# The end of a two-layer block: who finishes the last eight tiles of the feed-forward, and how the last store is issued

## The chip, the cores and the metric

One NeuronCore of a Trainium2 chip runs the whole program. The metric is the device time of one execution in microseconds (us), as the median of several executions. The engines are TensorE (PE in the rows, its weight loads PEld), VectorE (DVE), ScalarE (ACT), GpSimd (POOL) and SyncE (SP, which here only issues DMAs). Each engine takes its instructions strictly in the order in which they are written.

## The reference, cut to what matters

Two transformer-like layers on 1024 tokens of width 1024, all in float32. The change touches only the very end of the second layer, the feed-forward and its norm:

```python
h = rmsnorm(x, pre_ffn_norm[l])
f = (silu(h @ ffn_w_gate[l]) * (h @ ffn_w_up[l])) @ ffn_w_down[l]
x = x + rmsnorm(f, post_ffn_norm[l])      # f * 1/sqrt(mean(f*f) + eps) * weight
```

## The kernel before

The tokens lie in eight tiles of 128. `layer2_ffn` computes the down product as seven block products of a Strassen-like scheme, each with 11 steps, so 77 steps in all (`STEPS_B`, numbered 0 to 76). A step loads two blocks of 128x512; ScalarE rounds both to the short format (`split_step`, lines 3699 and 3700, which raise `r_hi`), VectorE makes the two remainders (`low_step`, line 3982 and the one after it, shown in the profile as line 3742, which raise `r_lo`), and TensorE runs three groups of four matmuls. A group needs both high parts, the second group the first remainder, the third group the second remainder (lines 4163 to 4168). For steps 0 to 73 the order is step by step. The last three steps (74, 75, 76) are run tile by tile: nine matmuls for tile 0, then nine for tile 1, and so on (lines 4170 to 4178, semaphore `tile_done`). Tile 0 thus needs the splits and remainders of all three last steps.

Tiles 4 to 7 of the output (`OUT_ORDER` puts them first) get their last sums from product 5, on VectorE during steps 69 to 72. Tiles 0 to 3 get theirs from the last product, when `tile_done` says so. For each tile the work of the norm is then:

- the last sum, out of PSUM, on VectorE (line 4054, in the profile 3742, written to `features_T`, which the code calls `f`);
- the square and its sum along the row on ScalarE (`square`, line 3704), and the mean on VectorE (`mean`, line 4011);
- the multiplication by the norm weights on VectorE in halves of 512 columns (`weighted`, and line 4057 for the last half; out and in are `features_T`, the other input is `ff_gain`);
- the square root on ScalarE (`root`, line 3723), the reciprocal on VectorE (`inverse`, line 4016);
- the finish: scaling by the reciprocal and adding the residual, one instruction on VectorE over 1024 columns (`finish`, line 4024, x = f * r + x);
- the store of 512 KB by SyncE (line 3590), in the order `STORE_ORDER`.

ScalarE's order at the end is: both splits of a step, then a square or a root where one is due, then the splits of the next step. VectorE's is: the remainders of a step, then a sum, a mean, a weighting. `finish(0)` stands between the remainders of step 72 and those of step 73. All other finishes come after the remainders of step 76. GpSimd has done nothing since the middle of the feed-forward's start (line 4083).

Of the kernel before, what the change touches and what calls it, by code (L numbers as in the profile page):

```python
# [22 lines left out]
D = 1024  # L23
# [3369 lines left out]
def layer2_ffn(nc, block, mixed, W, B, G, U0, hT_hi, hT_lo, feat, st, x_in, g_post, out, a_dram, w_dram):  # L3393
# [4 lines left out]
    with ExitStack() as ctx:  # L3398
# [50 lines left out]
        def ring_raw(n):  # L3449
# [10 lines left out]
        r_here = [sem(f"r_here{s}") for s in range(R)]  # L3460
        r_hi, r_lo, step_done, tile_done = (sem(n) for n in ("r_hi", "r_lo", "step_done", "tile_done"))
        p1_b, evac_b = sem("p1_b"), sem("evac_b")
        x_here, sq_a, sq_b, ms, rt, scaled, x_new = (
            sem(n) for n in ("x_here", "sq_a", "sq_b", "ms", "rt", "scaled", "x_new"))
        x_t = x_in.rearrange("(t p) d -> t p d", p=P)
        out_t = out.rearrange("(t p) d -> t p d", p=P)

# [19 lines left out]
        FRESH = (True, True, False, True, True, False, False)  # L3487
        TILE_STEPS = 3
        OUT_ORDER = [4, 5, 6, 7, 0, 1, 2, 3]
        STORE_ORDER = [4, 5, 0, 6, 1, 7, 2, 3]  # L3490
        SCALED = [8, 10, 13, 16, 12, 15, 18, 20]

        def in_order(eng, start, pair, end):
            start()
# [8 lines left out]
        def _(sp):  # L3503
# [73 lines left out]
            def end():  # L3577
                for n in range(STEPS_B):
                    load_step(n)
                    if n == 7:  # L3580
                        spill(LAST, 0)
                    if n == 12:
                        sp.wait_ge(prod, 7 * H0 + 14 * LAST)
                        sp.dma_start(gain[:], g_post.to_broadcast([P, D])).then_inc(x_here, 16)
                    if n >= 13 and n % 2 and n < 13 + 2 * NT:
                        t = (n - 13) // 2
                        sp.dma_start(x[:, t, :], x_t[t]).then_inc(x_here, 16)
                for n, t in enumerate(STORE_ORDER):
                    sp.wait_ge(x_new, n + 1)
                    sp.dma_start(out_t[t], x[:, t, :]).then_inc(stored, 16)  # L3590
                sp.wait_ge(stored, 32 * PAIRS + 16 * NT)

            in_order(sp, start, pair, end)

# [1 line left out]
        def _(act):  # L3596
# [123 lines left out]
            def root(n):  # L3720
                t = OUT_ORDER[n]
                act.wait_ge(ms, n + 2)
                act.activation(st[:, t, 4:5], st[:, t, 3:4], ACT.Sqrt).then_inc(rt, 1)

            def end():
                for n in range(STEPS_B):
                    split_step(n)
                    p, t = divmod(n - PAIRS - 3, PAIRS)
                    if p >= 0 and t < 4:
                        piece(p, t)  # L3730
                    if p == 5 and 2 <= t < 6:
                        root(t - 2)
                for t in range(4):
                    act.wait_ge(evac_b, B_C12 + t + 1)
                    square(f[:, t, HALF:], t, 2, sq_b)
                    root(4 + t)

            in_order(act, start, pair, end)

        @block.vector  # L3740
        def _(dve):
# [271 lines left out]
            def inverse(n):  # L4013
                t = OUT_ORDER[n]
                dve.wait_ge(rt, n + 1)
                dve.reciprocal(st[:, t, 5:6], st[:, t, 4:5]).then_inc(scaled, 1)

            def weighted(t, at):
                TT(f[:, t, at:at + HALF], f[:, t, at:at + HALF], gain[:, at:at + HALF], ALU.mult).then_inc(scaled, 1)

            def finish(n):
                t = OUT_ORDER[n]
                dve.wait_ge(scaled, SCALED[n])
                dve.scalar_tensor_tensor(x[:, t, :], f[:, t, :], st[:, t, 5:6], x[:, t, :], ALU.mult, ALU.add).then_inc(x_new, 1)  # L4024

            def end():
                c12(1, LAST, 0)
                for k in (3, 1, 2, 4):
                    own_sum(k, LAST, 0)
                for n in range(R, STEPS_B):  # L4030
                    low_step(n)
                    p, t = divmod(n - PAIRS - 3, PAIRS)
                    if p >= 0 and t < 4:
                        piece(p, t)
                    if p == 4 and 4 <= t < 8:
                        dve.wait_ge(sq_a, t + 1)
                        weighted(t, HALF)
                    if p == 4 and t == 8:
                        dve.wait_ge(sq_a, NT)
                        dve.tensor_scalar(st[:, :, 1:2], st[:, :, 0:1], 1.0 / D, EPS, ALU.mult, ALU.add).then_inc(ms, 1)  # L4040
                        dve.wait_ge(ms, 1)
                    if p == 5 and 1 <= t < 5:
                        mean(t - 1)
                        weighted(3 + t, 0)
                    if p == 5 and t == 3:
                        inverse(0)
                        finish(0)
                for t in range(5):
                    if 1 <= t < 4:
                        inverse(t)  # L4050
                        finish(t)
                    if t < 4:
                        dve.wait_ge(tile_done, t + 1)
                        TT(f[:, t, HALF:], banks[0][t], u2_b[:, t, :], ALU.add).then_inc(evac_b, 1)
                    if t:
                        mean(3 + t)
                        TT(f[:, t - 1, HALF:], f[:, t - 1, HALF:], gain[:, HALF:], ALU.mult).then_inc(scaled, 1)
                        inverse(3 + t)
                        finish(3 + t)

            in_order(dve, start, pair, end)

# [1 line left out]
        def _(pool):  # L4064
# [16 lines left out]
            TT(own[0], own_block(0, 1), own_block(0, 0), ALU.subtract).then_inc(own_done, 1)  # L4081
            pool.wait_ge(own_done, 3)
            TT(own[2], own_block(1, 0), own[0], ALU.subtract).then_inc(own_done, 1)

        @block.tensor
        def _(pe):
# [249 lines left out]
```

## Time and profile before

| what | value |
|---|---|
| time, median of 3 runs | 2253.35 us (2251.65 to 2255.38) |
| span of the profiled execution (first to last instruction) | 2258.5 us |
| TensorE busy | 2216.4 us, 98% of the span |
| VectorE busy | 1581.9 us, 70% |
| ScalarE busy | 914.2 us, 40% |
| GpSimd busy | 263.5 us, 12% |
| mean granted TensorE clock | 0.990 |

The busy shares are means over the whole program. The profile gives the span of the profiled execution and no other time for it; that span is 5.15 us longer than the median of the runs. The times in the rows below count from the start of the span.

### The profile page before, as it was taken

Reading aid. Unit: us, or ns where it says so; the run is one execution under the profiler, and the core shown is the slowest. Engines: PE = TensorE matmul, PEld = TensorE weight load, DVE = VectorE, ACT = ScalarE, POOL = GpSimd, SP = SyncE. Lnnn points to the kernel's source line nnn. Section 1 sums busy time; section 2 is a strip of 40 time slices with the busy share of each in tenths; the row PEclk is TensorE's granted clock in tenths of the full one; section 3 lists DMA queues with packets and bytes.
Section 4 is the critical chain, followed back from the end, with each engine's and each line's share of the span. In section 5 each row is a group of like instructions: output and inputs, shape, how many; then the busy total and the mean of one; then the engine's idle time right before and its main releaser. Section 6 shows DMA issues by size and latency. Waiting matters only on the chain. (4 is left out here: it accounts for less than half of the span.)

```text
span 2258.5 us, 34288 instructions
## 1 busy us (share of the span) xinstructions
PE 2216.4 (98%) x13052; PEld 1823.0 (81%) x13052; DVE 1581.9 (70%) x2212; ACT 914.2 (40%) x1672; POOL 263.5 (12%) x266
## 2 busy tenths in 40 slices
PE   8999999999999999999999989999999999999997
PEld 7888888888888887887877777887888888888886
DVE  5657678876665545657687788887798777765557
ACT  5443544343343321243344445555533333324444
POOL 0222232100000000001232222322020000000000
PEclk9999999999999999999999989999999999999999
DMA  4111111144333264433233442323235444448655
GB/s 152 47 38 58 37 56 38 66 147 157 116 114 111 86 261 175 150 111 122 85 112 112 150 141 72 107 93 112 96 131 191 163 158 163 158 156 299 214 181 184
DMA packets 106952, 289.06 MB, mean 128 GB/s; under 512 B 9692, under 2 KB 35388, under 8 KB 102332
## 3 DMA queue, kind: packets, MB, share of 16 engines
q1 hardware_dynamic: 106812, 287.14, 36.2%
q8 instruction: 94, 1.54, 0.3%
q14 instruction: 46, 0.38, 0.1%
HBM read 205.01 MB, written 82.10 MB: 127 GB/s over the span
## 5 line engine op out<-in xcount | busy, mean ns | idle before, releaser
L124 PE MATMUL psG<-h_hi,w_hi 128*128 128x512 f32 (+1 forms) x624 | 164.4, 395 | 2.1 <-DVE features_T L1875 1.6
L124 PE MATMUL psG<-h_hi,w_lo 128*128 128x512 f32 (+1 forms) x624 | 161.6, 391 | 0.0
L124 PE MATMUL psG<-h_lo,w_hi 128*128 128x512 f32 (+1 forms) x624 | 161.4, 392 | 0.0
L455 POOL TENSOR_TENSOR sb_w<-sb_left 128x128 f32<-128x128 f32 (+3 forms) x96 | 96.9, 1014 | 320.3 <-DVE sb_left L582 320.3
L124 PEld LDWEIGHTS psG<-h_hi,w_hi 128*128 128x128 f32 x624 | 109.9, 188 | 23.7 <-DVE features_T L1875 2.9
L124 PEld LDWEIGHTS psG<-h_hi,w_lo 128*128 128x128 f32 x624 | 111.4, 188 | 20.2 <-DVE w_lo L155 0.2
L124 PEld LDWEIGHTS psG<-h_lo,w_hi 128*128 128x128 f32 x624 | 111.1, 188 | 20.1 <-issue 0.5
L582 DVE TENSOR_TENSOR_SCAN sb_left<-sb_left 128x128 f32<-128x128 f32 (+3 forms) x96 | 102.7, 1078 | 2.1 <-ACT sb_left L468 1.4
L150 ACT CAST w_hi<-w_raw 128x1024 fp32r<-128x1024 f32 x48 | 50.3, 1049 | 120.0 <-PE psG L124 61.7
L155 DVE TENSOR_TENSOR w_lo<-w_raw,w_hi 128x1024 fp32r<-128x1024 f32 x48 | 58.6, 1222 | 55.0 <-ACT w_hi L150 55.0
L2024 POOL TENSOR_TENSOR features_T<-m_bias_both 128x512 f32<-128x512 f32 x10 | 16.8, 1675 | 680.3 <-DMA m_bias_both<-in_proj_pairs 633.0
L590 DVE TENSOR_TENSOR sb_w_lo<-psT,sb_w_hi 128x512 fp32r<-128x512 f32 (+1 forms) x80 | 50.0, 624 | 61.8 <-ACT sb_w_hi L476 61.3
L468 ACT ACTIVATE sb_left<-psA 128x128 f32<-128x128 f32 (+3 forms) x96 | 47.1, 491 | 101.1 <-PE psA L124 52.6
L476 ACT CAST sb_w_hi<-psT 128x512 fp32r<-128x512 f32 (+1 forms) x80 | 43.5, 543 | 87.2 <-PE psT L721 87.2
L1051 ACT ACTIVATE features_T<-features_T 128x512 f32<-128x512 f32 x54 | 34.1, 632 | 90.0 <-DVE features_T L1128 89.5
L3742 DVE TENSOR_TENSOR h_ffn_lo<-ff_raw_up,h_ffn_hi 128x512 fp32r<-128x512 f32 x49 | 33.7, 689 | 41.4 <-ACT h_ffn_hi L3700 20.8
L1912 DVE SCALAR_TENSOR_TENSOR features_T<-features_T,p_par 128x1024 f32<-128x1024 f32 x42 | 59.9, 1426 | 2.7 <-ACT features_T L1776 1.7
L3742 DVE TENSOR_TENSOR features_T<-ff_y,features_T 128x512 f32<-128x512 f32 x50 | 34.4, 689 | 35.7 <-PE ff_y L124 35.7
L3742 DVE TENSOR_TENSOR w_lo<-ff_raw_up,w_hi 128x512 fp32r<-128x512 f32 x39 | 26.9, 691 | 45.3 <-ACT w_hi L3700 45.3
L124 PE MATMUL m_ps<-m_w_hi,m_a_hi 128*128 128x512 f32 x128 | 54.0, 432 | 0.4 <-ACT m_raw L2450 0.4
L3608 ACT CAST ff_a_hi<-features_T 128x512 fp32r<-128x512 f32 x40 | 24.5, 623 | 69.7 <-PE psH L124 29.5
L1128 DVE TENSOR_TENSOR features_T<-mg_y,features_T 128x512 f32<-128x512 f32 x45 | 31.0, 689 | 29.6 <-PE mg_y L124 29.1
(657 smaller groups left out, 5949.8 us busy)
## 6 DMA issues: line engine op xcount, KB each, us to landing
w_raw<-in_units SPq DMA_DIRECT2D x76, 512.0 KB, 4.3
w_raw<-hidden_blocks SPq DMA_DIRECT2D x77, 256.0 KB, 2.9
merge_gates<-features_T SPq DMA_DIRECT2D x12, 1024.0 KB, 6.7
merge_gates<-merge_gates SPq DMA_DIRECT2D x12, 1024.0 KB, 4.8
features<-features_T SPq DMA_DIRECT2D x24, 512.0 KB, 3.8
w_spare<-in_units SPq DMA_DIRECT2D x22, 512.0 KB, 4.4
down_sums<-w_spare SPq DMA_DIRECT2D x22, 512.0 KB, 3.3
hidden_blocks<-features_T SPq DMA_DIRECT2D x11, 1024.0 KB, 3.9
```

What stands on the lines that cost most here:

```text
L124: return pe.matmul(out, lhs, rhs, start=first, stop=last, skip_group_check=True)
L150: act.copy(self.hi[c % 2][:] if dest is None else dest, self.raw[c % 2][:]).then_inc(self.hi_done, 1)
L155: dve.tensor_tensor(self.lo[c % 2][:] if dest is None else dest, self.raw[c % 2][:], hi.bitcast(F32), ALU.subtract).then_inc(self.lo_done, 1)
L455: pool.tensor_tensor(w, left_chunk(S, 1), left_chunk(S), ALU.subtract).then_inc(w_ready, 1)
L468: act.activation(left_chunk(S), A[:, 0:row_chunk(S)[1]], ACT.Sigmoid, scale=-1.0).then_inc(keep_done, 1)
L476: act.copy(w_hi[n % 2][:, 0:m], wT[n % 2][:, 0:m]).then_inc(w_hi_done, 1)
L582: dve.tensor_tensor_scan(back, back, back, start, ALU.mult, ALU.min).then_inc(scan_done, 1)
L590: dve.tensor_tensor(w_lo[n % 2][:, 0:m], wT[n % 2][:, 0:m], w_hi[n % 2][:, 0:m].bitcast(F32), ALU.subtract).then_inc(w_lo_done, 1)
L1051: act.activation(dst, src, func).then_inc(gated, 1)
L1128: TT = lambda o, a, b, op: dve.tensor_tensor(o, a, b, op)
L1912: dve.scalar_tensor_tensor(acc[r], raw[r][:, t:t + T], par[:, c, t:t + 1], acc[r], ALU.mult, ALU.add).then_inc(step if t else conv_out, 1)
L3742: TT = lambda o, a, b, op: dve.tensor_tensor(o, a, b, op)
```

## The change

Finishing is divided among three engines. For the first five tiles in `OUT_ORDER` (4, 5, 6, 7 and 0) ScalarE multiplies the weighted tile by the reciprocal root in place (`times_root`) and GpSimd adds it to the residual (`pool.tensor_tensor`, add). VectorE finishes the tiles 1, 2 and 3 (`result`, n = 5, 6, 7). For tiles 0 to 3 the second half of the weighted tile goes to the buffer `v_b` (free by then), so that the weighting (`last_sum`) can stand right behind the last sum while ScalarE still squares the unweighted half; these tiles are therefore finished in two halves of 512 columns. The stores go out in `OUT_ORDER`, the last one as two stores of 256 KB. On ScalarE `times_root(0)` to `times_root(3)` stand behind the splits of steps 73, 74, 75 and 76 in turn, on VectorE `inverse(0)` to `inverse(3)` behind the remainders of steps 72 to 75.

```diff
-        STORE_ORDER = [4, 5, 0, 6, 1, 7, 2, 3]
-        SCALED = [8, 10, 13, 16, 12, 15, 18, 20]
+        BY_POOL, POOL_PARTS = 5, (1, 2, 3, 4, 6)
+        def parts(n):
+            return [(f[:, OUT_ORDER[n], :], slice(0, D))] if n < 4 else [(f[:, OUT_ORDER[n], 0:HALF], slice(0, HALF)), (v_b[:, OUT_ORDER[n], :], slice(HALF, D))]
+        def result_ready(eng, n):
+            eng.wait_ge(inverted, n + 1)
+            eng.wait_ge(scaled, 5 + n)
...
@@ SyncE
+                for n in range(NT - 1):
+                    if n < BY_POOL:
+                        sp.wait_ge(pool_new, POOL_PARTS[n])
+                    else:
+                        sp.wait_ge(vector_new, 2 * (n - BY_POOL) + 2)
+                    t = OUT_ORDER[n]
                     sp.dma_start(out_t[t], x[:, t, :]).then_inc(stored, 16)
+                t = OUT_ORDER[NT - 1]
+                sp.wait_ge(vector_new, 2 * (NT - BY_POOL) - 1)
+                sp.dma_start(out_t[t][:, 0:HALF], x[:, t, 0:HALF]).then_inc(stored, 16)
+                sp.wait_ge(vector_new, 2 * (NT - BY_POOL))
+                sp.dma_start(out_t[t][:, HALF:], x[:, t, HALF:]).then_inc(stored, 16)
...
@@ ScalarE
+            def times_root(n):
+                result_ready(act, n)
+                for src, _ in parts(n):
+                    act.mul(src, src, st[:, OUT_ORDER[n], 5:6]).then_inc(by_root, 1)
...
                     if p == 5 and 2 <= t < 6:
                         root(t - 2)
+                    if p == 5 and 4 <= t < 8:
+                        times_root(t - 4)
                 for t in range(4):
                     act.wait_ge(evac_b, B_C12 + t + 1)
                     square(f[:, t, HALF:], t, 2, sq_b)
                     root(4 + t)
+                    if t == 1:
+                        times_root(4)
...
@@ VectorE
+            def last_sum(t):
+                dve.wait_ge(tile_done, t + 1)
+                TT(f[:, t, HALF:], banks[0][t], u2_b[:, t, :], ALU.add).then_inc(evac_b, 1)
+                dve.wait_ge(evac_b, B_C12 + t + 1)
+                TT(v_b[:, t, :], f[:, t, HALF:], gain[:, HALF:], ALU.mult).then_inc(scaled, 1)
...
-                    if p == 5 and t == 3:
-                        inverse(0)
-                        finish(0)
-                for t in range(5):
-                    if 1 <= t < 4:
-                        inverse(t)
-                        finish(t)
-                    if t < 4:
-                        dve.wait_ge(tile_done, t + 1)
-                        TT(f[:, t, HALF:], banks[0][t], u2_b[:, t, :], ALU.add).then_inc(evac_b, 1)
-                    if t:
-                        mean(3 + t)
-                        TT(f[:, t - 1, HALF:], f[:, t - 1, HALF:], gain[:, HALF:], ALU.mult).then_inc(scaled, 1)
-                        inverse(3 + t)
-                        finish(3 + t)
+                    if p == 5 and 3 <= t < 7:
+                        inverse(t - 3)
+                def result(n):
+                    result_ready(dve, n)
+                    for src, at in parts(n):
+                        dve.scalar_tensor_tensor(x[:, OUT_ORDER[n], at], src, st[:, OUT_ORDER[n], 5:6], x[:, OUT_ORDER[n], at],
+                                                 ALU.mult, ALU.add).then_inc(vector_new, 1)
+                for t in range(4):
+                    last_sum(t)
+                    if t:
+                        inverse(3 + t)
+                    if t == 3:
+                        result(6)
+                    mean(4 + t)
+                    if t == 2:
+                        result(5)
+                inverse(7)
+                result(7)
...
@@ GpSimd
+            pool.wait_ge(x_here, 16 * (NT + 1))
+            for n in range(BY_POOL):
+                for k, (src, at) in enumerate(parts(n)):
+                    pool.wait_ge(by_root, POOL_PARTS[n] - len(parts(n)) + k + 1)
+                    TT(x[:, OUT_ORDER[n], at], x[:, OUT_ORDER[n], at], src, ALU.add).then_inc(pool_new, 1)
```

## Rows read from the trace of the kernel before

**Rows 1.** The chain that ended last, at its end: start us, us, what.
```profile
2240.48 0.69 DVE features_T L3742
...
2254.19 1.28 DVE ff_x L4024
```
**Rows 2.** Groups of instructions by line, last 30 us: busy us, mean ns, idle before.
```profile
L4024 DVE SCALAR_TENSOR_TENSOR ff_x<-features_T,small_cols,ff_x 128x1024 f32<-128x1024 f32 x8 | 10.3, 1285 | 0.3
L3742 DVE TENSOR_TENSOR features_T<-features_T,ff_gain 128x512 f32<-128x512 f32 x6 | 4.1, 684 | 0.0
...
L3704 ACT ACTIVATE ff_junk<-features_T 128x512 f32<-128x512 f32 x5 | 3.1, 621 | 5.2 <-DVE features_T L3742 5.2
```
**Rows 3.** Timeline of ScalarE near the last splits: start us, us.
```profile
2234.23 0.61 ACT L3699 CAST ff_a_hi<-w_raw 128x512 fp32r<-128x512 f32 x1
...
2235.71 0.20 ACT L3723 ACTIVATE small_cols<-small_cols 128x1 f32<-128x1 f32 x1 [0.35 <-DVE small_cols L4011]
...
2237.37 0.62 ACT L3700 CAST w_hi<-ff_raw_up 128x512 fp32r<-128x512 f32 x1
```
**Rows 4.** Timeline of VectorE near the last remainders: start us, us.
```profile
2234.92 0.69 DVE L3742 TENSOR_TENSOR w_lo<-w_raw,w_hi 128x512 fp32r<-128x512 f32 x1
2235.52 0.15 DVE L4011 SCALAR_TENSOR_TENSOR small_cols<-small_cols 128x1 f32<-128x1 f32 x1
...
2239.21 0.68 DVE L3742 TENSOR_TENSOR w_lo<-w_raw,w_hi 128x512 fp32r<-128x512 f32 x1
```
**Rows 5.** Timeline of TensorE, first tile of the last three steps.
```profile
2238.11 0.39 PE L124 MATMUL psH<-ff_a_hi 128*128 128x512 f32 x1
...
2239.94 0.50 PE L124 MATMUL psH<-w_hi,w_lo 128*128 128x512 f32 x1
```
**Rows 6.** Last store: SyncE's issue, and GB/s in 40 slices of 2255.4 to 2260.
```profile
2255.50 0.33 SPq L3590 DMA_DIRECT2D out<-ff_x  x1
GB/s 321 0 0 0 0 0 0 0 463 463 427 321 499 392 463 356 463 427 285 0 0 0 0 0 0 0 0 0 0 0 0 0 0 0 0 0 0 0 0 0
```
**Rows 7.** ScalarE over 1024 columns, by line: ns min/median/max.
```profile
L1776 ACT ACTIVATE features_T<-features_T,p_par x14: 1242/1246/1247, 1123.1 to 1269.6; 128x1024 f32<-128x1024 f32 x14
L1780 ACT ACTIVATE features_T<-features_T x14: 1059/1062/1065, 1132.4 to 1276.5; 128x1024 f32<-128x1024 f32 x14
```
**Rows 8.** GpSimd's line 4065: ns min/median/max of its instructions.
```profile
L4065 POOL TENSOR_TENSOR features_T<-features_T x4: 1295/1618/1737, 1689.2 to 1694.0; 128x512 f32<-128x512 f32 x4
```
**Rows 9.** Timeline of GpSimd at 380 to 420 us, line 455.
```profile
389.30 1.04 POOL L455 TENSOR_TENSOR sb_w<-sb_left 128x512 f32<-128x512 f32 x1 [2.42 <-DVE sb_left L582]
391.84 0.39 POOL L455 TENSOR_TENSOR sb_w<-sb_left 128x128 f32<-128x128 f32 x1 [1.50 <-DVE sb_left L582]
```
**Rows 10.** Timeline of GpSimd and VectorE side by side, 1180 to 1190 us.
```profile
1182.24 1.73 POOL L2024 TENSOR_TENSOR features_T<-m_bias_both 128x512 f32<-128x512 f32 x1
1183.09 1.96 DVE L1912 SCALAR_TENSOR_TENSOR features_T<-features_T,p_par 128x1024 f32<-128x1024 f32 x1 [0.27 <-ACT features_T L1776]
1184.04 2.16 POOL L2024 TENSOR_TENSOR m_bias_both<-m_bias_both 128x512 f32<-128x512 f32 x1
1185.08 3.52 DVE L1912 SCALAR_TENSOR_TENSOR features_T<-features_T,p_par 128x1024 f32<-128x1024 f32 x2
```
**Rows 11.** Timeline of VectorE beside GpSimd's work of rows 8.
```profile
1689.72 1.34 DVE L3742 TENSOR_TENSOR features_T<-features_T 128x512 f32<-128x512 f32 x1
...
1692.68 0.67 DVE L3742 TENSOR_TENSOR features_T<-features_T,ff_y 128x512 f32<-128x512 f32 x1
```
**Rows 12.** Stretches: length, busy us of each engine, then PEclk (granted clock), DMA, GB/s.
```profile
1284.00:1286.00 2.00, 0.74 (x4) 0.28 (x2) 0.69 (x1) 0.07 (x1) 0.00 (x0) 1.00 0.42 172
1286.00:1288.00 2.00, 0.33 (x2) 0.36 (x3) 0.78 (x4) 0.00 (x0) 1.09 (x5) 0.71 0.83 281
1288.00:1290.00 2.00, 2.00 (x11) 2.00 (x10) 0.00 (x0) 1.17 (x3) 1.86 (x3) 0.50 0.99 331
...
1294.00:1296.00 2.00, 2.00 (x25) 1.78 (x24) 1.01 (x2) 0.11 (x1) 0.40 (x1) 1.00 1.03 422
```

More of the change, by code:

```diff
@@ L3462, in layer2_ffn @@
         p1_b, evac_b = sem("p1_b"), sem("evac_b")
-        x_here, sq_a, sq_b, ms, rt, scaled, x_new = (
-            sem(n) for n in ("x_here", "sq_a", "sq_b", "ms", "rt", "scaled", "x_new"))
+        x_here, sq_a, sq_b, ms, rt, scaled, inverted, by_root, pool_new, vector_new = (
+            sem(n) for n in ("x_here", "sq_a", "sq_b", "ms", "rt", "scaled", "inverted", "by_root", "pool_new", "vector_new"))
         x_t = x_in.rearrange("(t p) d -> t p d", p=P)
@@ L3587, in end @@
                         sp.dma_start(x[:, t, :], x_t[t]).then_inc(x_here, 16)
-                for n, t in enumerate(STORE_ORDER):
-                    sp.wait_ge(x_new, n + 1)
-                    sp.dma_start(out_t[t], x[:, t, :]).then_inc(stored, 16)
-                sp.wait_ge(stored, 32 * PAIRS + 16 * NT)
+                for n in range(NT - 1):
[4 more added lines that the diff above has]
+                    t = OUT_ORDER[n]
+                    sp.dma_start(out_t[t], x[:, t, :]).then_inc(stored, 16)
+                t = OUT_ORDER[NT - 1]
[3 more added lines that the diff above has]
+                sp.dma_start(out_t[t][:, HALF:], x[:, t, HALF:]).then_inc(stored, 16)
+                sp.wait_ge(stored, 32 * PAIRS + 16 * NT + 16)
             in_order(sp, start, pair, end)
@@ L4015, in inverse @@
                 dve.wait_ge(rt, n + 1)
-                dve.reciprocal(st[:, t, 5:6], st[:, t, 4:5]).then_inc(scaled, 1)
+                dve.reciprocal(st[:, t, 5:6], st[:, t, 4:5]).then_inc(inverted, 1)
             def weighted(t, at):
                 TT(f[:, t, at:at + HALF], f[:, t, at:at + HALF], gain[:, at:at + HALF], ALU.mult).then_inc(scaled, 1)
[L4021 to L4024, printed above, removed]
+            def last_sum(t):
[3 more added lines that the diff above has]
+                TT(v_b[:, t, :], f[:, t, HALF:], gain[:, HALF:], ALU.mult).then_inc(scaled, 1)
             def end():
```

## The prediction
> **What bounds the kernel now.** I read the chain that ended last first. Until 2240.44 us it is TensorE (tile 0's last matmul, 2239.94 and 0.50) [rows 5], and from 2240.48 to 2255.47 (2254.19 and 1.28) it is VectorE alone, 15.0 us without a wait that matters [rows 1]. Behind it the last store is issued at 2255.50, and the span ends at 2258.5, 3.0 us later [rows 1, 6]. So the program has two bounds, one after the other: TensorE up to the first tile of the last three steps, then VectorE's finishing. The groups of the last 30 us say what the second consists of: eight finishes at 1285 ns, of which seven lie behind 2240.48 (one started earlier, inside the steps), and the weightings at 684 ns, as long as a last sum (0.69) [rows 1, 2]. VectorE starts the next instruction 0.09 us before the end of one (2234.92 and 0.69, the next at 2235.52) [rows 4], so a finish costs about 1.20 and a sum 0.60; I take the same overlap for ScalarE.
>
> Then I read the three engines just ahead of that point, since the change inserts work there. ScalarE ends its last split at 2237.99 (2237.37 and 0.62) [rows 3]. VectorE ends its last remainder at 2239.89 [rows 4]. TensorE starts the last matmul of tile 0 at 2239.94 [rows 5]. These three fit without play: the last remainder of step 76 ends 0.05 us before the matmul that needs it. Whatever makes a split or a remainder late makes TensorE late by as much, less what `finish(0)` gave back. TensorE's four tiles of nine matmuls follow at about 0.23 us a matmul (2238.11 to 2239.94 for eight), so 2.05 us a tile [rows 5].
>
> **What is removed.** VectorE loses five finishes of 1.20, four of them behind 2240.48: 4.8 us of its tail. The three that stay are cut in halves, two of about 0.60 for one of 1.20, which costs nothing. The weighting moves ahead of the mean, which hides ScalarE's square (621 ns) [rows 2] and costs nothing; the extra wait between sum and weighting is about 0.12 us a tile, 0.5 us in all. The last store in halves: 512 KB flow in 11 slices of 0.115 us, 1.27 us [rows 6]; with half of it gone ahead, between 0 and 0.63 us of the 3.0 go. I take 0.63, as the first half is issued one 0.60 earlier. By this alone the end would come about 5 us earlier.
>
> **What is added on ScalarE.** Four multiplications over 1024 columns stand between the splits. The rows of that width are 1062 ns and, with two operands taken per row, 1246 ns [rows 7]; less the overlap of 0.1, each holds the queue 0.96 to 1.15 us, and I take 1.0. Behind `times_root(0)` wait the splits of step 74, behind `times_root(1)` those of step 75, behind `times_root(2)` those of step 76. So the last split is 3.0 us late by this alone, at about 2241.0 for 2237.99, and the remainders of step 76 follow it to 2242.3 for 2239.89, since VectorE must wait for it: +2.4 us on tile 0. The 1.2 us from `finish(0)` are of no use, because VectorE waits for ScalarE. `times_root(4)` lies among the squares and roots, where ScalarE has room.
>
> **What is added on GpSimd, and what it does to VectorE.** Four adds over 1024 columns, two over 512. Only 512 columns are shown: 1.295 us at best on the same tensor [rows 8], 1.04 on another [rows 9]. From 128 columns (0.39) to 512 (1.04) it rises by 1.7 ns a column, so 1024 cost at least 1.9; twice 1.295 is 2.6 and the upper end. I take 2.4, on the line from 0.39 through 1.295, since that tensor is the one added here, and 1.3 for a half. SyncE takes its waits in order, so the stores of VectorE's tiles stand behind that of GpSimd's last half; in the sum below that half ends at 2255.8, ahead of VectorE's first tile (2257.1), so this costs nothing. Were it later than VectorE's last half, it would set the end.
>
> The question is whether VectorE keeps its pace meanwhile. The trace says that it doesn't. At 1183.09 VectorE starts an instruction with two inputs in SBUF while GpSimd is at work (from 1182.24); it takes 1.96 instead of 1.285. GpSimd's next one, started at 1184.04, takes 2.16 instead of 1.295, and the two of VectorE from 1185.08 take 3.52 for 2.49 [rows 2, 8, 10]. The excess is each time what the other had left to do: they take turns, whole instruction by whole instruction. At 1689.72 a remainder-like instruction takes 1.34 for 0.69, while one whose second input is in PSUM takes 0.67 under the same GpSimd work (1689.2 to beyond 1694.0) [rows 8, 11]. So remainders, weightings and finishes stand still while a GpSimd add runs, last sums don't.
>
> The Trainium skill says the same, and speaks against this change: the page "SBUF — State Buffer", section "Who interferes with whom", has a VectorE instruction with two SBUF inputs contend with a GpSimd instruction that reads SBUF, whoever is second being fully blocked. The trace agrees (1.34 us for 0.69). By "GPSIMD Engine Reference", section "Elementwise — side-by-side cycle accounting", an add over 2048 columns takes 4497 ns; half is an estimate of 2.25 us, by which the sum below would be 0.8 us smaller.
>
> **The sum, in order of time.** I lay the new order on the old times.
>
> 1. ScalarE: `times_root(0)` 2234.23 to 2235.3, splits of step 74 to 2236.35. GpSimd's first add runs from 2235.4 to 2237.85.
> 2. VectorE: remainders of step 73 to 2235.6 as before [rows 4]. `mean(3)` (0.15 us, but two inputs in SBUF) is due at 2235.5 and meets the add: done at 2238.0. For `root(3)` ScalarE waits until then, before 2235.71 [rows 3]. The weighting, `inverse(1)` and the remainders of step 74 follow to 2239.9.
> 3. ScalarE: `times_root(1)` 2238.7 to 2239.8, splits of step 75 to 2240.85, `times_root(2)` to 2241.85, splits of step 76 to 2242.9.
> 4. GpSimd's second add 2239.9 to 2242.3. First remainder of step 75 waits for it, to 2243.0. The third add, already waiting, takes its turn to 2245.3; the second remainder ends at 2246.0, those of step 76 at 2247.25.
> 5. TensorE: tile 0 is done at 2247.5 instead of 2240.44 (2239.94 and 0.50): **+7.1 us** [rows 5].
> 6. Tail of VectorE from there. Four sums, four weightings and six half finishes at 0.60 are 8.4; means, reciprocals and the waits between sum and weighting 1.3; turns of GpSimd's fourth add and its two halves 3.1; waits for ScalarE's roots about 1.1. That is 13.9 instead of 15.0, and 2.4 instead of 3.0 behind it: **-1.7 us**.
>
> Together +5.4 us on the span. The span of the profiled execution is 5.15 us above the median of the runs; I add the difference to the median: 2258.8 us.
>
> One thing is missing: between 2238 and 2247.5 TensorE would run only nine matmuls, about 2 us of work. In the trace it stood almost still for some 3 us from 1284.7; its clock fell from 1.00 to 0.50 (1.2 GHz) and came back some 6 us after it was busy again [rows 12]. I expect that here too. At half clock a tile takes 4.1; the three later tiles would be done at 2257.0 instead of 2253.7, and, as VectorE lags behind them anyway, the end is 2.1 later. That makes **+7.5 us, 2260.9 us**, which I forecast. With cheap adds (1.9) it is 2.0 to 2.3 less; with multiplications at 1.15 it is 2.3 more.
>
> **Rivals.**
>
> - *The turns hold, the clock doesn't fall*: TensorE gets a matmul every 2 or 3 us, which may suffice. 2258.8 us, and 2256.5 with cheap adds. For it: no row shows how often a lone matmul is enough. Against it: 2 us of work in 9.4 is about as little as in the 4 us from 1284 (0.74 and 0.33) [rows 12].
> - *No turns* (the other side): the adds run beside VectorE, as where its other input is in PSUM. Then only the multiplications delay tile 0, by 2.4, the last tile is done about 2.0 later, and the last half finish comes at 2253.9 for 2255.47: -1.6, with the store -2.2 us, 2251.2 us. It is decided by `mean(3)` at 2235.5: if that lasts 0.15 us, this rival is right. Against it: rows 10 and 11.
> - *The change does what it seems to be for*: neither ScalarE nor GpSimd delays a split or a remainder. TensorE's last tile is done as before, at 2246.6 (2240.44 and three times 2.05); sum, square, mean, root and reciprocal take about 2.1, the halves 1.3, the store 2.4: 2252.4, -6.1 us, 2247.3 us. Against it: ScalarE takes its queue in order, and its last split had 1.5 us of play (done at 2237.99, first needed by the seventh matmul of tile 0 at 2239.5) for a delay of 3.0 [rows 3, 5].
>
> **Numbers.** Turns with a falling clock 0.48 (2258.7 to 2263.3), turns at full clock 0.28 (2256.5 to 2261.1), no turns 0.15 (2251.2, 2253.5 if the clock falls in the shorter wait), the full gain 0.05, something unforeseen such as table loads of ScalarE 0.04. What this kernel's measurement tells from no change is 0.2%, 4.5 us: below 2248.85 or above 2257.85. Slower: nearly all of the first, three quarters of the second, the last: 0.71. Faster: the full gain, and a little of no turns: 0.07. Same: 0.22. The range 2253.0 to 2263.5 leaves out most of the no-turns case, the full gain and the worst.
>
> **What would show it.** In the profile after: `mean(3)` or the weighting behind it lasting over 2 us; remainders of steps 75 and 76 at 2 to 3 us; tile 0 done near 2247.5; a granted clock below 1.00 between 2240 and 2254; GpSimd adds at 2.4, and at 3.0 where they wait; the last store's second half issued some 2.4 us before the end. Wrong I am if remainders stay at 0.69 beside the adds, if an add costs well under 1.9, or if tile 0 is done before 2243.

## The result, and the profile after

Slower by about half a per cent: 2265.01 us, median of four executions (2261.35 to 2265.52), beside 2252.53 us before (2251.65 to 2255.38). The ratio is 1.0047, 95% interval 1.0032 to 1.0061. The forecast was 2260.9: the sign came out, but the median lies 1.5 us above the upper end of the range. The profile has to say whether the mechanism came out too.

The whole times don't compare well to a microsecond, because the same kernel reaches its end several us earlier or later. So I compare one stretch: from the first matmul of the last product to the end of the span. In the profiled executions it is 42.15 us before (2216.35 to 2258.5) and 51.24 us after (2211.36 to 2262.6): **+9.1 us** where the prediction's sum gave +7.5. These are the first matmuls of the last product, before and after:

```profile
2216.35 1.07 PE L124 MATMUL psH<-ff_a_hi 128*128 128x512 f32 x4
2211.36 1.07 PE L124 MATMUL psH<-ff_a_hi 128*128 128x512 f32 x4
```

Inside the stretch, the first last sum starts 24.13 us after the product's start before and 33.32 after (+9.2; forecast +7.1), and from that sum to the end it is 18.02 and 17.92 us (-0.1; forecast -1.7 from the work and +2.1 from the clock).

VectorE's timeline after, around the last remainders, says where the nine microseconds are (start us, us; the times count from the start of the span). Line 3767 is what was 3742.

```profile
2230.47 0.15 DVE L4036 SCALAR_TENSOR_TENSOR small_cols<-small_cols 128x1 f32<-128x1 f32 x1
2230.54 0.68 DVE L3767 TENSOR_TENSOR features_T<-features_T,ff_gain 128x512 f32<-128x512 f32 x1
...
2231.43 2.61 DVE L3767 TENSOR_TENSOR ff_a_lo<-ff_raw_up,ff_a_hi 128x512 fp32r<-128x512 f32 x1
2233.96 2.83 DVE L3767 TENSOR_TENSOR ff_a_lo<-w_raw,ff_a_hi 128x512 fp32r<-128x512 f32 x1
2236.72 0.15 DVE L4041 RECIPROCAL small_cols<-small_cols 128x1 f32<-128x1 f32 x1
2236.79 0.67 DVE L3767 TENSOR_TENSOR h_ffn_lo<-ff_raw_up,h_ffn_hi 128x512 fp32r<-128x512 f32 x1
...
2239.11 1.93 DVE L3767 TENSOR_TENSOR w_lo<-ff_raw_up,w_hi 128x512 fp32r<-128x512 f32 x1 [0.98 <-ACT w_hi L3716]
2240.96 2.83 DVE L3767 TENSOR_TENSOR w_lo<-w_raw,w_hi 128x512 fp32r<-128x512 f32 x1
2244.68 0.69 DVE L3767 TENSOR_TENSOR features_T<-psH,ff_u_b 128x512 f32<-128x512 f32 x1 [0.89 <-PE psH L124]
```

Before, every remainder took 0.68 or 0.69 [rows 4]. Now four of the six take 1.93 to 2.83 us: 7.4 us more in all. The two of step 75 between them still take 0.67 and 0.68. GpSimd's timeline over the same time tells which four these are:

```profile
2230.52 2.97 POOL L4095 TENSOR_TENSOR ff_x<-ff_x,features_T 128x1024 f32<-128x1024 f32 x1 [539.91 <-ACT features_T L3744]
...
2238.13 2.36 POOL L4095 TENSOR_TENSOR ff_x<-ff_x,features_T 128x1024 f32<-128x1024 f32 x1 [1.89 <-ACT features_T L3744]
```

Two adds lie behind one another from 2230.52 to 2236.24, and two from 2238.13 to 2243.24. The remainders of steps 74 and 76 fall into these two times, those of step 75 between them. The add at 2238.13 began with nothing in its way and took 2.36; the first took 2.97, the 2.36 and the 0.6 that the weighting at 2230.54 held. The Trainium skill's page "GPSIMD Engine Reference", section "Elementwise — side-by-side cycle accounting", led to an estimate of 2.25; the measured 2.36 decides, 0.04 below what the sum took.

On ScalarE the multiplications cost 1.14 and 1.15, and the third waits 3.33 us for a reciprocal that stands behind the slow remainders on VectorE; the splits of step 76 wait behind it.

```profile
2229.23 1.14 ACT L3744 ACTIVATE features_T<-features_T,small_cols 128x1024 f32<-128x1024 f32 x1
...
2236.90 1.15 ACT L3744 ACTIVATE features_T<-features_T,small_cols 128x1024 f32<-128x1024 f32 x1 [3.33 <-DVE small_cols L4041]
...
2238.46 0.61 ACT L3716 CAST w_hi<-ff_raw_up 128x512 fp32r<-128x512 f32 x1
```

TensorE's first tile is starved by VectorE and, once, by ScalarE; its last matmul starts 1.95 us after the engine fell idle, and now takes 0.80 for 0.50 [rows 5]:

```profile
2233.11 0.39 PE L124 MATMUL psH<-ff_a_hi 128*128 128x512 f32 x1
2234.09 0.50 PE L124 MATMUL psH<-ff_a_lo,ff_a_hi 128*128 128x512 f32 x1 [0.59 <-DVE ff_a_lo L3767]
2236.85 0.50 PE L124 MATMUL psH<-ff_a_hi,ff_a_lo 128*128 128x512 f32 x1 [2.25 <-DVE ff_a_lo L3767]
...
2239.13 0.79 PE L124 MATMUL psH<-w_hi 128*128 128x512 f32 x1 [0.53 <-ACT w_hi L3716]
2241.09 0.80 PE L124 MATMUL psH<-w_lo,w_hi 128*128 128x512 f32 x1 [1.17 <-DVE w_lo L3767]
2243.84 0.80 PE L124 MATMUL psH<-w_hi,w_lo 128*128 128x512 f32 x1 [1.95 <-DVE w_lo L3767]
```

The stretches show why (length, busy time of TensorE, weight loads, VectorE, ScalarE, GpSimd, then the granted clock, DMA share, GB/s). TensorE was busy at most 1.30 us of each 2 us from 2234 to 2244, and its clock went from 1.00 (2.4 GHz) to 0.50 (1.2 GHz), as in [rows 12]. It came back only some 5 us after TensorE was fully busy again:

```profile
2234.00:2236.00 2.00, 0.50 (x1) 0.19 (x1) 2.00 (x2) 0.00 (x0) 2.00 (x1) 1.00 0.64 262
...
2238.00:2240.00 2.00, 1.30 (x3) 0.47 (x2) 1.02 (x3) 2.00 (x4) 1.87 (x1) 0.74 0.17 70
2240.00:2242.00 2.00, 0.80 (x1) 0.29 (x1) 2.00 (x2) 0.13 (x1) 2.00 (x2) 0.50 0.35 145
2242.00:2244.00 2.00, 0.16 (x1) 0.16 (x1) 1.79 (x1) 0.00 (x0) 1.24 (x1) 0.50 0.29 117
2244.00:2246.00 2.00, 2.00 (x5) 1.61 (x6) 1.29 (x2) 0.60 (x2) 0.00 (x0) 0.50 0.64 262
2246.00:2248.00 2.00, 2.00 (x6) 1.52 (x6) 0.25 (x2) 0.32 (x3) 0.00 (x0) 0.50 0.00 0
2248.00:2250.00 2.00, 2.00 (x8) 1.58 (x7) 1.45 (x4) 0.72 (x2) 0.00 (x0) 0.70 0.00 0
2250.00:2252.00 2.00, 2.00 (x11) 1.65 (x10) 1.16 (x4) 1.74 (x4) 0.92 (x1) 1.00 0.00 0
```

SyncE issues the last two stores 3.04 and 2.4 us before the end at 2262.6; before, the one store was issued 3.0 us ahead of the end [rows 6]:

```profile
2259.56 0.33 SPq L3604 DMA_DIRECT2D out<-ff_x  x1
2260.22 0.33 SPq L3606 DMA_DIRECT2D out<-ff_x  x1
```

### The profile page after: what moved, and what is told of

It reads as the page before. It is cut to its first block and busy times, and to the rows that moved or that the text cites. A ratio compares the mean times of both kernels' runs of the same rounds, so it can differ in the third digit from the quotient of the medians.

```text
span 2262.6 us, 34308 instructions
## 1 busy us (share of the span) xinstructions
PE 2212.5 (98%) x13052; PEld 1817.9 (80%) x13052; DVE 1585.9 (70%) x2210; ACT 919.5 (41%) x1678; POOL 278.3 (12%) x272
## 5 line engine op out<-in xcount | busy, mean ns | idle before, releaser
L4095 POOL TENSOR_TENSOR ff_x<-ff_x,features_T 128x1024 f32<-128x1024 f32 (+1 forms) x5 | 12.1, 2443 | 549.6 <-ACT features_T L3744 549.6
L3624 ACT CAST ff_a_hi<-features_T 128x512 fp32r<-128x512 f32 x40 | 24.5, 623 | 69.7 <-PE psH L124 29.5
```

## The experiments

S0 is the start of the first last sum, counted from the start of the last product; the tail is what follows up to the end of the span. All in us, from one profiled execution each:

| kernel | S0 | tail | stretch |
|---|---|---|---|
| before | 24.13 | 18.02 | 42.15 |
| changed | 33.32 | 17.92 | 51.24 |
| 1: GpSimd only writes | 26.23 | 14.48 | 40.71 |
| 2: no multiplications | 32.25 | 16.63 | 48.88 |
| 3: adds late | 26.23 | 21.92 | 48.15 |
| 4: multiplications late | 24.25 | 21.68 | 45.93 |
| 5: VectorE finishes all | 24.84 | 16.56 | 41.40 |
| 6: TensorE kept busy | 33.17 | 16.23 | 49.40 |
| 7: two finishes early | 25.07 | 16.15 | 41.22 |
| 8: adds in quarters | 27.34 | 18.11 | 45.45 |
| 9: adds in eighths | 26.54 | 23.89 | 50.43 |
| changed again | 33.31 | 17.96 | 51.27 |
| before again | 24.14 | 17.97 | 42.11 |

The last two rows say how far such a difference can be trusted: within 0.1 us.

**1. GpSimd writes, but reads nothing.** Two fills of 1024 columns stand in place of each add over 1024, one of 512 in place of each half, so the residual of five tiles is left out.

```diff
-                    TT(x[:, OUT_ORDER[n], at], x[:, OUT_ORDER[n], at], src, ALU.add).then_inc(pool_new, 1)
+                    spare = (hT_hi, hT_lo)[k][:, 1 + n, :].bitcast(F32)
+                    if n < 4:
+                        pool.memset(hT_lo[:, 1 + n, :].bitcast(F32), 0.0)
+                        pool.memset(spare, 0.0).then_inc(pool_new, 1)
+                    else:
+                        pool.memset(spare[:, 0:HALF], 0.0).then_inc(pool_new, 1)
```

> Leaves out the residual of five tiles: GpSimd fills unused buffers with zeros (two fills of 1024 columns per tile, some 1 us each by the 0.52 us of 512 columns) at the places of its adds, so that it is busy but reads nothing; ScalarE's multiplications stay. Measure: the stretch from the first matmul of the last product to the end of the span (42.15 us before, 51.24 after the change), and the start of the first last sum in it (24.1 and 33.3). Theory (GpSimd's reading and VectorE take turns): remainders of steps 74 to 76 at 0.69, first sum at 26 to 27, stretch 40 to 42.5. Rival (ScalarE's multiplications between the splits do it): first sum at 31 or later, stretch 48 or more. Second rival (GpSimd at work slows VectorE whatever it does): remainders over 1.5.

Measured: S0 26.23, stretch 40.71. VectorE's timeline of this kernel, at the remainders of step 74:

```profile
2230.47 0.69 DVE L3767 TENSOR_TENSOR ff_a_lo<-ff_raw_up,ff_a_hi 128x512 fp32r<-128x512 f32 x1
2231.07 0.68 DVE L3767 TENSOR_TENSOR ff_a_lo<-w_raw,ff_a_hi 128x512 fp32r<-128x512 f32 x1
```

And GpSimd's at the same time:

```profile
2230.42 0.96 POOL L4121 MEMSET h_ffn_hi<- 128x1024 f32 x1
```

A remainder that runs beside a GpSimd fill keeps its 0.69 us. So it is not GpSimd's being at work that holds VectorE up; it is its reading. The Trainium skill states this on the page "SBUF — State Buffer", section "Who interferes with whom": a VectorE instruction with two SBUF inputs contends with a GpSimd instruction that reads SBUF, and not with one that only writes there. This run agrees (0.68 and 0.69), the changed kernel too (1.93 to 2.83). What ScalarE's multiplications cost by themselves can be read here as well: S0 is 2.1 us later than before, where the prediction took 2.4. And without the readings the rest of the change would have gained 1.4 us on the stretch. So reading adds in place of fills cost 10.5 us (51.24 less 40.71), with the fallen clock in it (experiment 6), and GpSimd's work here is also a little shorter (two fills of 0.96 for an add of 2.36).

**2. No multiplications.** ScalarE leaves out the scaling of the five tiles; GpSimd waits for the reciprocals instead.

```diff
             def times_root(n):
-                result_ready(act, n)
-                for src, _ in parts(n):
-                    act.mul(src, src, st[:, OUT_ORDER[n], 5:6]).then_inc(by_root, 1)
+                pass
...
-                    pool.wait_ge(by_root, POOL_PARTS[n] - len(parts(n)) + k + 1)
+                    result_ready(pool, n)
```

> Leaves out the scaling of five tiles: ScalarE's multiplications are gone, GpSimd's adds wait for the reciprocals and weights instead. Theory (turns): remainders still at 2 to 3 us, first sum at 31 to 33 (24.1 before, 33.3 after the change), stretch 47.5 to 49.5. Rival (multiplications between the splits): first sum at 24, stretch 42 or less.

Measured: S0 32.25, stretch 48.88. Four remainders at 1.92, 2.85, 2.84 and 2.84 us, one for each add; this is the second of them, and the add beside it:

```profile
2234.99 2.85 DVE L3765 TENSOR_TENSOR ff_a_lo<-w_raw,ff_a_hi 128x512 fp32r<-128x512 f32 x1
2234.56 2.73 POOL L4093 TENSOR_TENSOR ff_x<-ff_x,features_T 128x1024 f32<-128x1024 f32 x1 [1.98 <-DVE small_cols L4039]
```

Taking the multiplications away gives back 1.1 of the 9.2 us; the adds alone keep tile 0 late.

**3. The adds wait until VectorE has made its last remainder.**

```diff
             pool.wait_ge(x_here, 16 * (NT + 1))
+            pool.wait_ge(r_lo, 2 * STEPS_B)
```

> GpSimd's adds wait for the last remainder of step 76; all else as in the change. Theory (turns): remainders at 0.69, first sum at 26 to 27 (the multiplications alone), but the six adds (about 12 us) then take turns with VectorE's weightings and finishes, so that the stretch is still 46 to 49, not below the 42.15 of before. Rival (only the remainders' delay matters, the tail is shorter by the work given away): stretch 39.5 to 41.

Measured: S0 26.23, as with fills, so the remainders are free. But the tail is 4.0 us longer than in the changed kernel. VectorE's timeline in it, below GpSimd's row of four adds that run from 2238.42 to 2248.71:

```profile
2238.42 10.29 POOL L4095 TENSOR_TENSOR ff_x<-ff_x,features_T 128x1024 f32<-128x1024 f32 x4 [546.52 <-DVE w_lo L3767]
2239.60 1.77 DVE L3767 TENSOR_TENSOR ff_v_b<-features_T,ff_gain 128x512 f32<-128x512 f32 x1
2241.29 2.35 DVE L4036 SCALAR_TENSOR_TENSOR small_cols<-small_cols 128x1 f32<-128x1 f32 x1
2243.57 0.68 DVE L3767 TENSOR_TENSOR features_T<-psH,ff_u_b 128x512 f32<-128x512 f32 x1
2244.28 2.23 DVE L3767 TENSOR_TENSOR ff_v_b<-features_T,ff_gain 128x512 f32<-128x512 f32 x1
```

The last sum, with one input in PSUM, takes its 0.68. The weightings wait, and the mean, an instruction over one single column, takes 2.35 us for 0.15: its two inputs lie in SBUF, so it waits for a whole add.

**4. The multiplications stand behind all the splits** (and so the adds come later too).

```diff
-                    if p == 5 and 4 <= t < 8:
-                        times_root(t - 4)
+                for n in range(4):
+                    times_root(n)
```

> ScalarE's four multiplications stand behind the splits of step 76, so GpSimd starts later by itself; all else as in the change. Theory (turns): at most one remainder of step 76 meets an add, first sum at 24 to 26.5, the tail behind it 19 to 20 for 18.0, stretch 44.5 to 46.5. Rival (multiplications were the cause): stretch 40 to 42.

Measured: S0 24.25, as good as before; tail 21.68, somewhat over what I expected (19 to 20), stretch 45.93, within it. The means take 2.35 and 2.22 here too. So this place for the adds isn't free either: with tile 0 untouched the change still loses 3.8 us.

**5. The rest of the change alone.** VectorE finishes all eight tiles, with the weightings behind the last sums and the last finish and store in halves; ScalarE's multiplications and GpSimd's adds are gone.

```diff
+                    if p == 5 and t == 3:
+                        result(0)
...
                 for t in range(4):
+                    if t == 0:
+                        result(1)
                     last_sum(t)
                     if t:
                         inverse(3 + t)
-                    if t == 3:
-                        result(6)
+                    result((2, 3, 4, 5)[t])
                     mean(4 + t)
-                    if t == 2:
-                        result(5)
+                result(6)
...
```

> Of the change only the rest is kept: weightings right behind the last sums, the second half of the finish from its own buffer, the last finish and the last store in halves; VectorE finishes all eight tiles, ScalarE multiplies nothing and GpSimd adds nothing. Turns theory: the rest is worth nothing. First last sum 24.1 to 24.7 us after the start of the last product (24.13 in the kernel before), stretch from the start of the last product to the end 41.5 to 42.5 us (42.15 before): the store in halves gives 0.6 back, the waits between sum and weighting and the cut finishes take 0.5 to 1.0. Rival (the order of the tail is worth 2 us by itself and the two other engines only hide it): stretch 40 us or less.

Measured: stretch 41.40, 0.75 us less than before, a shade under the expected 41.5 to 42.5, and far from the rival's 40. S0 is 0.7 later, 0.1 over what I expected, because one more finish (`result(1)`) stands before it, and the tail is 1.5 shorter. The rest is worth a little, and cannot be seen in whole times.

**6. TensorE kept busy.** 33 matmuls that nobody reads (by `UNREAD` and by the profile's count, 13085 for 13052; the expectation says 23) stand ahead of tile 0's waits in the changed kernel.

```diff
+                UNREAD = {0: (0, 3, 9), 1: (0, 1, 2), 2: (3, 6, 9)}
+                pe.wait_ge(evac_b, B_C21 + 4)
+                def unread(m):
+                    for _ in range(m):
+                        a_h, _, b_h, _ = ring(STEPS_B - TILE_STEPS)
+                        weights_pass(pe, banks[1][0], a_h[:, 0:P], b_h, True, True)
...
+                            unread(UNREAD[n - STEPS_B + TILE_STEPS][0])
                             pe.wait_ge(r_hi, 2 * n + 2)
                         for k in range(3):
                             if t == 0 and k:
+                                unread(UNREAD[n - STEPS_B + TILE_STEPS][k])
                                 pe.wait_ge(r_lo, 2 * n + k)
```

> The changed kernel, with 23 further matmuls on TensorE whose product is never read, put ahead of the waits of tile 0 in the last three steps. If the fallen clock costs what the prediction said (about 2 us): granted clock 1.00 in every 2 us window from 2230 us to the end, first last sum within 0.5 us of the changed kernel's 33.3 us after the start of the last product, last tile some 6.2 us behind tile 0 instead of 8.5, stretch 49 to 49.5 us for 51.24. Rival (VectorE lags so far behind that the clock costs nothing): the clock holds and the stretch stays at 51 us.

Measured: clock 1.00 in every stretch up to TensorE's last matmul. These are two; the same distance behind the product's start (2240.86 to 2244.86) the changed kernel had 0.50:

```profile
2246.00:2248.00 2.00, 1.89 (x8) 1.39 (x8) 2.00 (x2) 0.00 (x0) 2.00 (x1) 1.00 0.64 262
2248.00:2250.00 2.00, 1.80 (x9) 1.14 (x8) 1.41 (x2) 0.00 (x0) 0.53 (x1) 1.00 0.31 129
```

S0 33.17 for 33.32, the last matmul of the last tile 6.26 us behind that of tile 0 (8.73 in the changed kernel), stretch 49.40 for 51.24. So the fallen clock cost 1.8 us, nearly all in the tail, and idle TensorE was not the cause of the rest. In this tail two instructions of VectorE, a weighting and a mean, still wait for GpSimd's two halves:

```profile
2254.51 1.65 DVE L3767 TENSOR_TENSOR ff_v_b<-features_T,ff_gain 128x512 f32<-128x512 f32 x1
2256.16 1.14 DVE L4036 SCALAR_TENSOR_TENSOR small_cols<-small_cols 128x1 f32<-128x1 f32 x1
```

**7. Two finishes early, nothing for GpSimd.** Built on the kernel before: roots one step earlier, two finishes inside the last steps instead of one, last finish and store in halves.

```diff
...
-                    if p == 5 and 2 <= t < 6:
-                        root(t - 2)
+                    if p == 5 and 1 <= t < 5:
+                        root(t - 1)
...
-                    if p == 5 and t == 3:
-                        inverse(0)
-                        finish(0)
+                    if p == 5 and 2 <= t < 4:
+                        inverse(t - 2)
+                        finish(t - 2)
...
```

> The kernel before with no work for GpSimd and no multiplication on ScalarE: roots one step earlier, two finishes instead of one inside the last three steps where VectorE waits for ScalarE and TensorE, last finish and last store in halves. If VectorE's place in the queue is what counts: first last sum 24.1 to 24.6 us after the start of the last product, stretch 40.3 to 41.0 us for 42.15 (one more finish hidden, 1.2 us, half of the last store ahead, 0.6 us); on the whole time some 1.5 us or 0.07%, so no change that the times can tell. Rival (the earlier root delays the splits behind it, as a wait on ScalarE's queue): first last sum over 25 us, stretch 42 us or more.

Measured: 2251.33 us beside 2252.92, ratio 0.9994, interval 0.9984 to 1.0004: no difference that can be told. The stretch of 41.22 lies between the two expectations, with a piece of each: the tail is 1.9 us shorter, as expected (1.2 and 0.6), but S0 is 25.07, 0.9 later, as the rival said. ScalarE's timeline shows it:

```profile
2226.89 0.20 ACT L3724 ACTIVATE small_cols<-small_cols 128x1 f32<-128x1 f32 x1 [1.49 <-DVE small_cols L4012]
```

The early root waits 1.49 us for a mean that stands behind the finish and two remainders on VectorE, and the splits of steps 74 to 76 stand behind the root.

**8 and 9. The adds in pieces of 256 columns (below) and of 128.**

```diff
-  TT(x[:, OUT_ORDER[n], at], x[:, OUT_ORDER[n], at], src, ALU.add).then_inc(pool_new, 1)
+  for c in range(0, at.stop - at.start, 256):
+      one = x[:, OUT_ORDER[n], at.start + c:at.start + c + 256]
+      added = TT(one, one, src[:, c:c + 256], ALU.add)
+  added.then_inc(pool_new, 1)
```

> The changed kernel, each GpSimd add cut into pieces of 256 columns (four for a tile, two for a half). If the two engines take turns by the instruction, a remainder waits for one piece and no longer for a whole add. A piece lies between 0.39 (128 columns) and 1.295 us (512), so some 0.65 to 0.7: a remainder that meets it lasts 1.2 to 1.4 us, none lasts over 1.6 (in the changed kernel four lasted 2.6 to 2.9), ScalarE's wait for the reciprocal shrinks from 3.3 to about 1 us, the first last sum comes 28 to 30 us after the start of the last product instead of 33.3. The work itself is not less, so the tail meets the rest of it: stretch 45 to 49 us for 51.24, still over the 42.15 of the kernel before. Rival (GpSimd keeps the path as long as it has work queued): remainders stay at 2.6 to 2.9, first last sum at 33.

> The same in pieces of 128 columns (eight for a tile, four for a half), 0.39 us each where nothing blocks them, so 3.1 us a tile instead of 2.4. Turns by the instruction: a remainder that meets one lasts 0.9 to 1.1 us, first last sum 27.5 to 29.5 us after the start of the last product; the dearer adds run into the tail, stretch 45 to 50 us. If it comes out shorter than with quarters, the length of a blocking instruction counts more than the sum of GpSimd's work; if longer, the sum does. Rival as with quarters: remainders at 2.6 to 3.1, first last sum at 33 or later.

Measured: stretch 45.45 and 50.43 for 51.24; the second is a shade over the expected 45 to 50. VectorE's timeline with quarters:

```profile
2227.54 0.93 DVE L3767 TENSOR_TENSOR ff_a_lo<-ff_raw_up,ff_a_hi 128x512 fp32r<-128x512 f32 x1
2228.40 1.23 DVE L3767 TENSOR_TENSOR ff_a_lo<-w_raw,ff_a_hi 128x512 fp32r<-128x512 f32 x1
```

No remainder lasts over 1.23 us with quarters or over 0.95 with eighths, so the turns are by the instruction, and GpSimd doesn't hold the path while it has work queued. S0 falls to 27.34 and 26.54, both below what I expected (28 to 30, 27.5 to 29.5): with eighths next to nothing of the adds is left on the way to tile 0 (26.23 with fills). But the pieces now run on for longer. A piece of 256 columns takes 0.72 us where nothing blocks it and 1.17 in the median, one of 128 at least 0.45. With quarters GpSimd is done at 2246.0, ahead of VectorE's last half (2250.24). With eighths it is done at 2256.1, 3.2 us after VectorE (2252.94), and the stores of VectorE's tiles have waited in SyncE's queue behind that of GpSimd's last half:

```profile
2256.16 1.57 SPq L3601 DMA_DIRECT2D out<-ff_x  x3
2257.78 1.14 SPq L3604 DMA_DIRECT2D out<-ff_x  x1
2258.96 1.16 SPq L3606 DMA_DIRECT2D out<-ff_x  x1
```

That is the case that the prediction named for SyncE's order ("were it later than VectorE's last half, it would set the end"); 2 MB then leave at once. So both counted: the length of a blocking instruction for tile 0, and the sum of GpSimd's work for the end. VectorE itself was even done sooner with eighths: 40.47 us after the product's start, for 42.79 with quarters.

**Both kernels again.**

> The changed kernel as it is, a second time on another day of the chip's life. If the loss lies in the end alone, the stretch from the start of the last product to the end is again 51.2 us, within 0.3, whatever the whole time; the start of the last product may move by several us with the place where the granted clock falls between 1280 and 1380 us. If part of the loss lies ahead of the end, the last product starts at 2211 us or later in every execution of the changed kernel, for about 2208.5 that the spans of the kernel before give (span less 42.15).

> The kernel before as it is. Its profiled execution started the last product at 2216.35 us, which I take for an early loss of clock and no property of the end: expected are a start between 2207 and 2213 and again a stretch of 42.15 us, within 0.3. If the stretch differs by over 1 us, the comparisons of single executions in this study are worth less than they seem.

Measured: the stretches repeat to 0.03 and 0.04 us. The ratio does too: 2265.91 us for seven executions of the changed kernel, 2253.72 for ten of the one before, 1.0045 (1.0032 to 1.0058). The last product starts at 2213.63 and 2207.79 us. Most of this difference arises where the granted clock falls in the middle of the program: up to 1362 us the same instructions of the two executions start within 0.7 us of one another, from 1380 on they are 5.2 us apart. This is that stretch in the changed kernel (columns as above):

```profile
1360.00:1380.00 20.00, 17.95 (x134) 14.27 (x134) 15.74 (x33) 7.77 (x22) 1.67 (x2) 0.66 0.12 40
```

The same of the kernel before:

```profile
1360.00:1380.00 20.00, 18.28 (x172) 15.61 (x173) 17.73 (x42) 9.49 (x27) 4.22 (x7) 0.91 0.11 41
```

In the executions whose last product starts at 2207 to 2208 (experiments 4, 7 and 8, and the kernel before here) the clock in this stretch is 0.91 or 1.00; in those at 2211 to 2214 (both of the changed kernel, experiments 2, 3, 5, 9) it is 0.66. The two latest starts are 2216.35, in the first profile of the kernel before, and 2216.50, in experiment 6. There the clock had fallen earlier, as this stretch of the first profile of the kernel before shows:

```profile
1340.00:1360.00 20.00, 20.00 (x188) 17.66 (x187) 11.05 (x24) 7.87 (x23) 8.02 (x11) 0.62 0.18 61
```

Experiment 1 (2210.39) lies between, with 0.94 and 0.89 in the two stretches from 1300 to 1340. So the start goes with where and for how long the clock falls, far ahead of what the diff touches. Spans less the stretch put the changed kernel's start between 2207.6 and 2214.6 us in its eleven executions, which the first theory allows and the second doesn't (2211 or later in each).

## Why the prediction was right, and where its sizes were off

- **What bounds the kernel**: right. TensorE up to tile 0, then VectorE; what was lost within the stretch entered through those two.
- **What is removed, and the tail**: the total came out by luck, as two errors cancel. With the clock held (experiment 6) the tail is 16.23 us for 18.02, -1.8 where the sum had -1.7, and VectorE's part of it 13.8 us for 13.9. But the sum had 3.1 us of turns in that part, and 10.8 of the rest. With fills (experiment 1) the same part takes 12.1, so the turns were only 1.6, because the fourth add had come ahead of tile 0, and the rest was 1.3 longer. In it half finishes follow one another at 0.67, not 0.60, and VectorE waits twice for 0.4 us for a tile of TensorE. So what was removed gave 3.5 us on the tail (14.48 for 18.02) where about 5 was forecast.
- **ScalarE's multiplications**: 1.14, and 1.05 to the start of the next, for 1.0 taken; +2.1 on S0 alone (experiment 1) for +2.4. Small.
- **GpSimd's adds**: 2.36 for 2.4 taken, halves 1.30 for 1.3.
- **Turns**: right, by experiments 1, 3, 8 and 9. Only instructions of VectorE with two SBUF inputs wait, only for GpSimd instructions that read, and for one instruction at a time.
- **The placing in steps 2 to 4** is the term of the sum that was mis-sized. Step 2 let `mean(3)` meet the first add. It started at 2230.47, 0.05 us ahead of the add, and the weighting slipped in before it too; the add's turn came at the first remainder of step 74. By then the second add was ready, as the second multiplication needed only `inverse(1)`, which was no longer late, and took the next turn. So step 74 lost 1.92 and 2.14 us over 0.69, where the prediction had 2.4 on the mean and none behind it; `inverse(2)` came late, ScalarE waited 3.33 us for it, and the third multiplication ended 26.69 us after the product's start for 25.50 forecast (2241.85 less 2216.35). Step 75 went free, step 76 lost 1.24 and 2.14 (forecast: 1.5 and 2.4 on step 75, nothing on step 76). All four adds thus stood in the way of tile 0, where the sum had three and left the fourth to the tail. VectorE's last remainder ends 32.43 us after the product's start for 30.90 forecast, 1.5 later. Another 0.6 comes behind it: the last matmul ends 0.85 us after that remainder. The sum had 0.25 there, though the kernel before shows 0.55; the other 0.3 are the fallen clock. Sum: tile 0 +9.2 for +7.1.
- **The clock**: right. It fell, and cost 1.8 us (experiment 6) for 2.1 forecast.
- **The discriminator of the no-turns rival was wrongly put.** "If `mean(3)` lasts 0.15 us, this rival is right": it lasted 0.15, and the rival is false. The test hung on an order of two instructions that the sum itself put 0.1 us apart. Of the broader signs most were there: adds at 2.4 and 3.0, a clock below 1.00, the second half of the store 2.4 us before the end, and remainders at 2 to 3 us, but in steps 74 and 76 and not in 75 and 76.
- **The whole time**: the median is 4.1 us over the forecast. Of this 1.6 is the stretch (9.1 for 7.5); 3.4 lies ahead of the last product, where the sum had nothing, as the stretch explains only 9.1 of the 12.5 us between the medians; and the median before turned out 0.8 lower than the 2253.35 from which the sum started. The repeat has the gap again, 12.2 us. The product's start scatters by 7 to 9 us from execution to execution of one kernel, with the place where the clock falls. By spans less the stretch it was 2212.3 us in the median of eleven executions of the changed kernel and 2209.0 in that of 23 of the kernel before. The diff changes no instruction ahead of the last product. The clock of 0.66 from 1360 to 1380 us is in six of the ten profiles of the changed kernel and its variants and in none of the other three, too few to tell; whether these 3 us are chance was not settled.

## What to carry to other kernels

Work that is handed to GpSimd is not off VectorE's path if it reads SBUF: ask which of VectorE's instructions have two SBUF inputs, since each that meets such a GpSimd instruction waits for the rest of it, however small it is itself. Here 1.2 us of VectorE was traded for 2.36 us of the path that both need, and none of the three places tried won: it cost 9.1 us around tile 0 and 6.0 or 3.8 behind it (experiments 3 and 4). If such work must run on GpSimd, cut it into pieces about as long as VectorE's own instructions (the stretch fell by 5.8 us, though it stayed 3.3 above the kernel before), and let no queue put other stores behind it.

## What was not expected

- A mean over one column took 2.35 and 2.22 us beside adds, for 0.15: the price of a meeting is GpSimd's instruction, not VectorE's.
- The recorded start doesn't always tell who goes first. The add is recorded from 2230.52, the weighting from 2230.54, yet the weighting took 0.68 and the add 2.97 for 2.36. Why is not shown.
- Pieces of 128 columns cost at least 0.45 us on this tensor, not the 0.39 of [rows 9]; eight of them would be 3.6 us for an add of 2.36.
- The issue of a store took SyncE 1.14 us instead of 0.33 where five stores of 2 MB in all came at once (experiment 9).
